# Pairing narrow weight products of a six-branch decoder kernel from two column ranges

## The reference

```
def odd_layer(x, mem, ...):
    h = rms_norm(x, norm_g) @ w_in
    qkv_c, qkv_d, q_mem, gate = split_cols(h, ODD_SPLITS)
    ... sliding window attention on qkv_c
    o_d = dilated_attention(rope(q_d), rope(k_d), v_d)          # 6 heads of 128
    o_m = memory_attention(q_mem, mem, mem_norm_g, w_mem_kv)    # 4 heads of 128
    y = concatenate([o_c, o_d, o_m], axis=-1) * silu(gate)
    return x + y @ w_out

def hybrid_layer(x, ...):                                       # layers 2 and 3
    proj = rms_norm_2(x, norm_w) @ w_in
    (qa, ka, va, za, qi, ki, wi, ub, zb, qc, kc, vc, zc, gates) = split(proj)
    # widths 1024, 256, 256, 1024, 2048, 128, 16, 2048, 1024, 1024, 1024, 1024, 1024, 6144
    score = sum over 16 heads of relu(rope(qi) @ rope(ki).T) * wi    # picks the keys
    y_a = (dsa_attention(rope(qa), rope(ka), va, score) * silu(za)) @ w_a_out
    ... y_b a convolution branch of ub, y_c a stick-breaking attention of qc, kc, vc
    return x + (sum of sigmoid(gates) * y) @ w_out
```

## Time and profile before

| | |
|---|---|
| median of 3 runs | 3127.73 us (3127.19 to 3128.22) |
| profiled execution | 3127.91 us, its span 3126.1 us |
| PE busy | 3102.4 us, 99% of the span, 14692 matmuls |
| DVE busy | 2035.4 us, 65% |
| ACT busy | 1895.9 us, 61% |
| loads | 570.34 MB, mean 182 GB/s |

### The profile page before, as it was taken

One profiled execution on the slowest core, in us unless ns is written; L12 is line 12 of the kernel. 1 busy time (PEld: TensorE's weight loads), 2 busy tenths in 40 slices (PEclk: granted clock), 3 DMA queues, 4 the chain that ended last, 5 costly groups with the idle time before them and its releaser, 6 DMA issues. The chain is left out here.

```text
span 3126.1 us, 38344 instructions
## 1 busy us (share of the span) xinstructions
PE 3102.4 (99%) x14692; PEld 2599.3 (83%) x14692; DVE 2035.4 (65%) x3054; ACT 1895.9 (61%) x3019; POOL 7.1 (0%) x18
## 2 busy tenths in 40 slices
PE   8999999999999999999999999999999999999998
PEld 7888888888988888888888888888888888888886
DVE  6555564666555799997655555558999866555555
ACT  7677674678675557687744444444767776444443
POOL 0000000000000000000000000000000000000000
PEclk9999999999999999999999999999999999999999
DMA  8556665655566666565666666566565566666664
GB/s 310 167 147 179 176 201 169 208 158 154 163 183 203 178 183 175 171 176 156 175 189 195 194 192 193 182 189 177 175 182 162 155 181 177 194 207 193 193 187 149
DMA packets 301960, 570.34 MB, mean 182 GB/s; under 512 B 18097, under 2 KB 36673, under 8 KB 301393
## 3 DMA queue, kind: packets, MB, share of 16 engines
q1 hardware_dynamic: 297888, 557.65, 60.1%
q10 hardware_dynamic: 3040, 6.42, 0.6%
q0 software_dynamic: 848, 3.83, 0.3%
HBM read 565.73 MB, written 2.10 MB: 182 GB/s over the span
## 5 line engine op out<-in xcount | busy, mean ns | idle before, releaser
L134 DVE TENSOR_TENSOR wl<-raw,wh 128x1024 fp32r<-128x1024 f32 (+3 forms) x1088 | 1288.1, 1187 | 935.9 <-ACT wh L123 933.4
L123 ACT ACTIVATE wh<-raw 128x1024 fp32r<-128x1024 f32 (+3 forms) x1088 | 1119.5, 1031 | 1111.8 <-PE gp L108 1093.4
L108 PE MATMUL gp<-wh,Hh 128*128 128x512 f32 (+3 forms) x2400 | 921.2, 384 | 0.0
L108 PE MATMUL gp<-wh,Hl 128*128 128x512 f32 (+3 forms) x2400 | 911.4, 380 | 0.0
L108 PE MATMUL gp<-wl,Hh 128*128 128x512 f32 (+3 forms) x2400 | 911.2, 380 | 0.0
L108 PE MATMUL gp<-wh,Yh 128*128 128x512 f32 (+2 forms) x1952 | 761.5, 390 | 10.2 <-DVE wl L134 8.9
L108 PE MATMUL gp<-wh,Yl 128*128 128x512 f32 (+2 forms) x1952 | 755.5, 387 | 0.0
L108 PE MATMUL gp<-wl,Yh 128*128 128x512 f32 (+2 forms) x1952 | 755.4, 387 | 0.0
L108 PEld LDWEIGHTS gp<-wh,Hl 128*128 128x128 f32 x2400 | 451.3, 188 | 86.0
L108 PEld LDWEIGHTS gp<-wh,Hh 128*128 128x128 f32 x2400 | 451.6, 188 | 83.9 <-issue 1.7
L108 PEld LDWEIGHTS gp<-wl,Hh 128*128 128x128 f32 x2400 | 451.7, 188 | 82.4
(11 more groups left out here) (130 smaller groups left out, 1259.7 us busy)
## 6 DMA issues: line engine op xcount, KB each, us to landing
raw<-in_w_in SPq DMA_DIRECT2D x560, 512.0 KB, 3.7
raw<-in_ev_w_in SPq DMA_DIRECT2D x104, 512.0 KB, 3.8
raw<-in_od_w_in SPq DMA_DIRECT2D x80, 512.0 KB, 3.8
raw<-in_w_out SPq DMA_DIRECT2D x64, 512.0 KB, 4.1
raw<-in_ev_w_out SPq DMA_DIRECT2D x40, 512.0 KB, 3.7
raw<-in_od_w_out SPq DMA_DIRECT2D x36, 512.0 KB, 3.6
raw<-in_w_b_out SPq DMA_DIRECT2D x32, 512.0 KB, 3.9
raw<-in_w_a_out SPq DMA_DIRECT2D x32, 512.0 KB, 5.0
```

The lines of the kernel that those rows point to most:

```text
L108: return self.e.matmul(out, l, r, start=start, stop=stop)
L123: return self.e.activation(out, in_, func, **kw)
L134: return self.sketch(157 + size(a) * 1.042) if self.e is None else self.e.tensor_tensor(out, a, b, op)
```

## The change

Four edits. (1) In layers 2 and 3 `ki` takes the 256 columns of the values as a second range (400 in all), and `ka` keeps the 256 of the key. (2) Group 8 takes q and k in one Gemm of two ranges (512), v and gate in another, kind "vsilu". (3) Group 9 is not `carried`: in place of `flip_y` and `move_y`, PE transposes its rows (`turn_in`, eight transposes). (4) `evac` has rank 0, as `hi` and `lo`; at one time the one listed first goes first, and a Gemm's `evac` is listed ahead of the next Gemm's `hi`. A fill of two ranges is loaded by two DMAs. There are 1072 fills.

```
     def __init__(self, L, side, lo, w, c0, n, nk, kind, gid=None, part=0, also=()):
+        self.ranges = ((c0, n), *also)
+        self.n = sum(m for _, m in self.ranges)
...
+        qkv(group(7, 1, 0, "dil", 4, 4, 8), W, 1280, 2048, 2816, 5120, 512)
+        gr = group(8, 1, 1, "dil", 2, 2, 12)
+        gm = gemm(1, "H", 0, W, 1792, 256, 16, "nat", 8, also=((2560, 256),))
+        roped(gm, 0, 512, 128, rope_b)
+        turned(gm, self.region[1]["q"], 0, 4)
+        gr.turned.append(gm)
+        gr.v = gr.gate = gemm(1, "H", 0, W, 3328, 256, 16, "vsilu", 8, also=((5632, 256),))
         mem_heads(group(9, 1, 0, "mem", 4, 4, 14), W, 3584, 5888)
+        self.groups[9].carried = False
...
-            ki = gemm(L, "H", 0, W, C["ki"], 144, 16, "ki")
+            ki = gemm(L, "H", 0, W, C["ki"], 144, 16, "ki", also=((C["va"], 256),))
...
-            ka = gemm(L, "H", 0, W, C["ka"], 512, 16, "ka")
+            ka = gemm(L, "H", 0, W, C["ka"], 256, 16, "ka")
...
+        at = 0
+        for i, (c, n) in enumerate(gm.ranges):
+            src = gm.w[k:k + 256, c:c + n].rearrange("(t p) n -> p t n", p=128)
+            e.dma_start(P.raw[f % RAW][:, :, at:at + n], src).then_inc(*P.s_raw[f % RAW].up((f, i), 16))
+            at += n
...
         for i in range(0, gr.blocks, 2):
+            if not gr.carried:
+                add("pe", "turn_in", ("y", gr.gid), i)
...
         if s.name == "evac":
-            return 1
+            return 0
```

More of the change, by code:

```diff
@@ L295, with __init__ @@
 class Gemm:
-    def __init__(self, L, side, lo, w, c0, n, nk, kind, gid=None, part=0):
+    def __init__(self, L, side, lo, w, c0, n, nk, kind, gid=None, part=0, also=()):
         self.L, self.side, self.lo, self.w, self.c0, self.n, self.nk = L, side, lo, w, c0, n, nk
         self.kind, self.gid, self.part = kind, gid, part
+        self.ranges = ((c0, n), *also)
+        self.n = sum(m for _, m in self.ranges)
         self.turns, self.rope, self.copier, self.moved = [], None, "act", False
@@ L312, in __init__ @@
         self.turned = []
+        self.carried = True
 class Program:
@@ L599, in room @@
             return []
-        got = [self.v_in.at(("y", old, self.groups[old].blocks - 2)) if all_of_it else self.a_ymove.at((old, 3))]
+        got = [self.v_in.at(("y", old, self.groups[old].blocks - 2)) if all_of_it or not self.groups[old].carried
+               else self.a_ymove.at((old, 3))]
         if gid == 10:
@@ L723, in sources @@
             return [self.v_m.at((self.merge[n][2, c][1].g, 1))]
+        return [self.v_y.at((n, i), (n, i + 1))]
     def turned_at(self, gm):
@@ L768, in heads @@
             return [(col(r["q"], h), r["k"][:, 0:256])]
+        if gr.gid == 8:
+            return [(col(r["q"], h), col(r["q"], 2 + h))]
         return [(col(r["q"], h), col(r["k"], h))]
@@ L796, in v_at @@
         by = {"mla": gr.turned[2:], "mem": [self.mv_of[gr.L]] if gr.L < 2 else [], "swa": [self.swkv],
-              "dsa": [self.ka[gr.L - 2]]}.get(gr.kind, [gr.v])
+              "dsa": [self.ki[gr.L - 2]]}.get(gr.kind, [gr.v])
         return self.a_evac.at(*((gm.g, "end") for gm in by))
@@ L833, in raw @@
         k = 256 * j
-        src = gm.w[k:k + 256, gm.c0:gm.c0 + gm.n].rearrange("(t p) n -> p t n", p=128)
-        e.dma_start(P.raw[f % RAW][:, :, 0:gm.n], src).then_inc(*P.s_raw[f % RAW].up(f, 16))
+        at = 0
[3 more added lines that the diff above has]
+            at += n
     def store(n):
@@ L1136, in hi @@
             e.behind("load_first")
-        e.wait_ge(*P.s_raw[f % RAW].at(f))
+        e.wait_ge(*P.s_raw[f % RAW].at(*((f, i) for i in range(len(gm.ranges)))))
         if f >= SPLIT:
@@ L1166, in evac @@
             e.wait_ge(*P.nat.free((g, "t")))
-        if gm.gid is not None and kind in ("silu", "v", "ukv"):
+        if gm.gid is not None and kind in ("silu", "v", "vsilu", "ukv"):
             for w in P.room(gm.gid, False):
@@ L1204, in evac @@
                 i = e.activation(r["g"].rearrange("p (t c) -> p t c", t=2)[:, t, 0:n], p, ACT.Copy, scale=sc)
+            elif kind == "vsilu":
+                e.activation(b[:, t, 256:512], p[:, 256:512], ACT.Tanh, scale=P.rsh[:, t:t + 1])
+                e.activation(r["g"].rearrange("p (t c) -> p t c", t=2)[:, t, 0:256], p[:, 256:512], ACT.Copy,
+                             scale=P.rsh[:, t:t + 1])
+                i = e.activation(r["v"].rearrange("p (t c) -> p t c", t=2)[:, t, 0:256], p[:, 0:256], ACT.Copy, scale=sc)
             elif kind == "zb":
@@ L1215, in evac @@
                 e.activation(b[:, t, 0:128], p[:, 0:128], ACT.Copy, scale=sc)
-                i = e.activation(P.wi[:, t, :], p[:, 128:144], ACT.Copy, scale=sc)
-            elif kind == "ka":
-                e.activation(b[:, t, 0:256], p[:, 0:256], ACT.Copy, scale=sc)
+                e.activation(P.wi[:, t, :], p[:, 128:144], ACT.Copy, scale=sc)
                 for k in range(2):
@@ L1221, in evac @@
                         e.wait_ge(*w)
-                    i = e.activation(P.region[k]["v"][:, 128 * t:128 * t + 128], p[:, 256 + 128 * k:384 + 128 * k],
+                    i = e.activation(P.region[k]["v"][:, 128 * t:128 * t + 128], p[:, 144 + 128 * k:272 + 128 * k],
                                      ACT.Copy, scale=sc)
+            elif kind == "ka":
+                i = e.activation(b[:, t, 0:256], p[:, 0:256], ACT.Copy, scale=sc)
             elif kind == "swkv":
@@ L1283, in in_hi @@
             src = [P.turned_input(of, i + x) for x in range(2)]
-        elif of[0] == "y":
+        elif of[0] == "y" and P.groups[of[1]].carried:
             e.wait_ge(*P.a_ymove.at(*((of[1], a) for a in range(4))))
@@ L1463, in in_lo @@
                                    ALU.mult, ALU.subtract).then_inc(*P.v_in.up(key))
-        if not given and of[0] != "y":
+        if not given and not (of[0] == "y" and P.groups[of[1]].carried):
             P.bank.give(key, P.v_in, key)
@@ L1582, in gate @@
             r = P.region[P.groups[gm.gid].region]["g"].rearrange("p (t c) -> p t c", t=2)
-            x, t = r[:, :, 0:gm.n], P.nat.buf(g)[:, :, 0:gm.n]
+            a = 256 if gm.kind == "vsilu" else 0
+            x, t = r[:, :, 0:gm.n - a], P.nat.buf(g)[:, :, a:gm.n]
         e.scalar_tensor_tensor(x, t, 1.0, x, ALU.add, ALU.mult).then_inc(*P.v_gate.up(g))
@@ L1899, in heads @@
                     add(*s, gr.gid, h)
-        add("dve", "flip_y", gr.gid)
-        for a in range(4):
-            add("act", "move_y", gr.gid, a)
+        if gr.carried:
+            add("dve", "flip_y", gr.gid)
+            for a in range(4):
+                add("act", "move_y", gr.gid, a)
         for i in range(0, gr.blocks, 2):
+            if not gr.carried:
+                add("pe", "turn_in", ("y", gr.gid), i)
             add("act", "in_hi", ("y", gr.gid), i)
@@ L1991, in add_steps @@
         add("act", "evac", g)
-        if gm.kind in ("silu", "ubg", "zb"):
+        if gm.kind in ("silu", "vsilu", "ubg", "zb"):
             add("dve", "gate", g)
```

## The result

| | before | after |
|---|---|---|
| median | 3127.55 us (3126.78 to 3128.22, 7 runs) | 3117.20 us (3115.94 to 3117.88, 7 runs) |
| profiled execution, its span | 3127.91 us, 3126.1 us | 3116.99 us, 3115.2 us |
| ratio, 95% interval | | 0.9967, 0.9955 to 0.9979 |

The account below looks back on a forecast made before the run. PE was taken to bound the kernel, its span the sum of its instructions' start-to-start costs. Terms -2.55 - 7.18 + 0.88 - 1.6 gave -10.45 us, so 3117.5 us, range 3115.8 to 3121.0.

Parts of the forecast that it names:

- sign of being wrong: Forecast is wrong if 400-column matmuls cost over 0.19 us, or PE's waits sum to over 12 us.
- ki and ka, -7.18 us: In two layers, 96 matmuls each of 144 and 512 columns become 400 and 256, saving 3.59 us a layer.
- The floor: A matmul costs 13 ns plus 0.417 ns a column, but no less than near 0.11 us, so 144 columns overpay.
- Group 8, -2.55 us: In group 8, 384 matmuls of 256 columns at 0.1200 us become 192 of 512 at 0.2267, saving 2.55 us.
- The transposes, +0.88 us: Group 9's eight transposes add 0.88 us on PE; the moves they replace were hidden with 0.43 us to spare.
- evac ahead of hi, -1.6 us: At two places PE waits for ACT's evac, 0.81 and 0.84 us; evac's new rank recovers 1.6 us.
- new waits in part: Rival: the new order makes PE wait two to five us in places, giving 3119.5 to 3122.5; chance 0.20.
- the new wait in PE's queue: Group 9's transposes stand behind the third output fill; their input should be ready about 1 us before, adding nothing.
- Only columns count: Rival: pairings move the same columns and save nothing, neither per matmul nor by the floor, giving 3127.2 us; chance 0.03.
- the rule of the Trainium skill: A matmul's gap is N/2.4 + 2.5 ns, so both pairings together would save only 0.5 us.
- 400 columns cost as 512: Rival on ki's widened matmuls: 400 columns have the price of 512, giving 3126.2 us; chance 0.03.
- evac starves hi: Rival: evac holds up each hi until PE waits, at each of 151 Gemm ends, making the kernel slower; chance 0.03.

Follow-up runs that it names:

- the two kernels with transposes: The kernel before with group 9's transposes on PE alone, 3128.76 us, and with group 8's pairing as well, 3126.54 us.
- the two gate kernels: The changed kernel with each merge-gate matmul of 512 columns cut into two of 256, 3149.54 us, or into 384 and 128, 3260.40 us.
- merge gates in halves: The changed kernel with each 512-column matmul of the 24 merge-gate Gemms done as two of 256 columns: 3149.54 us.
- the second profile of group 8: The kernel before with group 8's pairing alone, profiled a second time: 3132.17 us, against 3128.44 us for its first profiled execution.

## Why the prediction was right

**What bounds the kernel** was read rightly: PE's starts set the span, and the three edits whose price stood in rows did what the rows said. Neither sign of being wrong appeared: 400 columns cost 0.180 us, and PE's waits sum to 9.8. "There is no clock to win back" holds for all but the start: the slices of the earlier trace rows are 78 us wide and don't show that the first steps ran at half pace: the first 40 took 11.61 us in the profile of before, where 40 x 0.227 is 9.08. No edit here touched that.

**ki and ka, -7.18 us.** Measured alone: -7.98, and -6.90 between the profiles without the start, a new wait of 0.5 us included. The estimate for 400 columns, 0.1809 us, met 0.180. The floor, which is the whole gain here since the number of matmuls stays, was confirmed at 208 and 128 columns.

**Group 8, -2.55 us.** Its price was right (-2.62 between the two kernels with transposes), and the 13 ns for a matmul held for 2304 matmuls more (14.0). But without the transposes the same pairing costs 2.4 us.

**The transposes, +0.88 us.** Right as a price (+0.91). The step "that cover was thin, but it held, so removing the moves gives nothing" was right for the kernel before and wrong for the one to be predicted. The cover of 0.43 us was spent by either of two other edits, evac's rank or the pairing, each alone; in their company the third edit is worth 4.4 us, not -0.9. That the sum came out in spite of this was luck: the change happened to have the one edit that removes the wait; a change with edits 1, 2 and 4 I would have forecast at 3116.6, and it takes 3121.6.

**evac ahead of hi, -1.6 us.** Mis-sized: 0.6 measured, 0.85 between the profiles without the start. Both waits went, with more room than forecast: the pair of Gemm 4 came free at 116.13 instead of 118.76, earlier by 2.6 us (0.4 of it since PE itself was ahead) and not by the 0.87 of one `hi`, because the table was loaded while ACT waited for PE. But part came back at other places, one of them a second wait of heads for smax (0.3 us). That loss is the "new waits in part" of the second rival, of a size of 1 us.

**The sum, -10.45 against -10.35.** That it met to 0.1 us is in part luck. The three other edits together gave -9.74 where the prediction's terms give -8.85, 0.9 more; evac's rank gave 1.0 less. The same two deviations stand between the profiles without the start (-9.59 and -0.85), so the start doesn't explain them, and the 0.7 to 0.9 us more isn't placed.

**Two DMAs for a fill** and **the new wait in PE's queue**: both hidden as argued. The latter had 917.00 - 915.69 = 1.3 us to spare, "about 1" by the forecast.

**The rivals.** "Only columns count" and the rule of the Trainium skill beside it are out by the two gate kernels, "400 columns cost as 512" by the row. "evac starves hi" did not occur at `hi`; the harm that evac's rank did alone was at the moves.

## What to carry to other kernels

Where one engine is full, price an edit by its start-to-start steps at each width, and look for the width below which the step stops falling: here joining narrow products paid mostly through that floor. A wait hidden by a few tenths of a microsecond is not a zero in a sum of several edits: ask of every thin cover what each of the other edits does to both of its ends, the supply and the demand. And a stall of some microseconds on TensorE can cost more than its length, since the clock may fall behind it; runs that spread more than those of their neighbour are a sign to take a second profile. Two profiles are best compared from a matmul behind the start, where here up to 1.5 us differ by chance.

## What was not expected of the hardware

In four profiles of kernels with a wait of 3.4 us, the granted clock behind it fell to 0.50 in three and stayed at 1.00 in one, the program of that one being the same as of one of the three. In none of the profiles without such a wait did it fall before PE's last matmul, though one of them has a wait of 1.5 us (merge gates in halves, at 56.44). At the start the column of the granted clock reads 1.00 while 5 to 12 steps of 512 columns take 0.43 us, as they do at 0.50 in the second profile of group 8; there the steps tell more than the column. Where 384 and 128 columns alternate the steps are uneven: the first of a narrow group is 0.06 us (1620.34 to 1620.40), the first of a wide one 0.23 (1619.75 to 1619.98) instead of 0.17, while the six add up to the sum of the prices.
